# Half-pair units in the recurrent layer of a four-layer network, their chunks beside the preparation of the next unit

## The chip, the cores and the metric

One core of one Trainium2 chip runs the whole network in one launch, all in float32 (large products are split into a rounded part and a remainder, three matmuls for one). The metric is the device time of one execution in microseconds (us). Before the change it is 4200.47 us, the median of 3 runs (4192.66 to 4201.72).

## The reference, cut to what matters

The part that the change touches is the mixing of the first layer. From the projection `p` of 1024 tokens it computes two things side by side: a recurrence over 8 heads of 64 channels, and attention of 8 heads over a band of nine 64-token chunks.

```python
w = -softplus(-(w0 + tanh(p_wd) @ w2)) - 0.5;  decay = exp(-exp(w))
a = sigmoid(a0 + p_ad @ a2)
kk = normalised(heads(k * k_k));  k = k * (1 + (a - 1) * k_a)
def step(state, inp):                 # over 1024 tokens, for each head
    sa = einsum('bhvk,bhk->bhv', state, a_t)
    state = state * w_t + sa[..., None] * b_t + v_t[..., None] * k_t
    return state, einsum('bhvk,bhk->bhv', state, r_t)
y = groupnorm(y) * lnx_g + lnx_b + sum(r * k * r_k) * v
...
y_a = y * silu(gate_a)
y_b = chunk_attention(q_b, k_b, v_b, att_bias) * silu(gate_b)
h + concatenate([y_a, y_b]) @ w_out
```

Shifted `p_r, p_k, p_v` (each token minus its predecessor, times a factor, added back) feed the recurrence. The three layers behind it are not touched.

## The kernel before, in words

The kernel writes five instruction queues by hand: PE (TensorE), DVE (VectorE), ACT (ScalarE), POOL (GpSimd) and SP, which issues DMAs. Each queue runs in order. Each engine's program is a Python generator that yields at the end of a round; `weave` takes one round of each of several generators in turn, `chain` puts generators one behind the other, and `pace(main, other, steps, rounds)` lays `steps` rounds of `other` evenly over `rounds` rounds of `main`. All engines use the same pattern, so that round n of one meets round n of the others; a semaphore wait in a round holds everything queued behind it on that engine.

The stage after the projection is `pace(*_rwkv(), *_band(), BAND_STEPS, RW_ROUNDS)`: the recurrence as the main part, the band attention as the other. Two heads (128 channels) are a pair, numbered c = 0 to 3. The recurrence works on 64-token chunks. For each pair it has these parts:

- `*_early(c)` (6 rounds): token shift of K, R and V, and the normalisation of kk. For pair 0 it lies in the projection, for the others beside the second half's chunks of the pair before.
- `*_late(c)` (6 rounds), alone: decay and `a` by two small matmuls and sigmoids, a scan along the tokens (L2677), three exponentials (L1728, L1733, L1736), some ten products on DVE, and transposes of the operands through PSUM. All operate on 1024 tokens at once.
- `*_factor(c, g)` (13 rounds) for each half g of the tokens: the chunk matrices (L796, L808), five doubling steps that invert them (L818, L826, L832, with copies and adds by ACT and DVE and masks by POOL), and from them WT and U0.
- `*_chunks(c, g)` (16 rounds): eight chunks in sequence. The state goes PE (L877) to DVE (L2811) to PE (L888) to DVE (L2818) and from there to the next chunk's L877. L897 and L900 give the output.
- `*_tail(c)` (10 rounds): the bonus of pair c, and normalisation, gate and transposes of the output of pair c-1.

They are put together so, for every engine: late(c); factor(c, 0) woven with tail(c); chunks(c, 0) woven with factor(c, 1); chunks(c, 1) woven with early(c+1). With the rounds that `weave` adds this is 6 + 14 + 17 + 17 = 54 rounds for a pair. The band attention has 4 pairs of 8 query tiles, each tile 6 rounds (192 in all): scores (L917), bias and maximum (L2837, L2848), exponential (L1824), division (L2858), transposes (L644), product with V (L938).

PSUM has eight banks. A `Banks` ring deals them out in order, and who opens one waits until what used it before has been copied out: the recurrence has four (`for_rw`), the band four (`for_band`). SP loads the rows that the projection spilled to memory: `sp_raw(c)` three raw rows for early(c), `sp_qk`, V and gates for the band; two of the four pieces of the output weight are loaded while the projection ends. After the stage, `*_even` finishes pair 3 and starts the output product (L656 to L658); there POOL splits the first weight piece (L3584) before it does the tail of pair 3 (L3497, L3502, L3508, L3515).

Of the kernel before, what the change touches and what calls it, by code (L numbers as in the profile page):

```python
# [151 lines left out]
def run(gen):  # L152
    for _ in gen:
        pass
# [24 lines left out]
def build(nc, T, out):  # L179
    ctx = ExitStack()  # L180
    with ctx:
# [97 lines left out]
        RW_ROUNDS, BAND_STEPS = 212, 192  # L279
# [27 lines left out]
        def ring(first, n):  # L307
# [4 lines left out]
        for_rw, for_band = ring(0, 4), ring(4, 4)  # L312
# [8 lines left out]
        rwv = area([(n, 1024) for n in ("A", "SIG", "CS", "EX", "T1")] + [("RA", 2048), ("BN", 1024)] +  # L321
                   [(n, 1024) for n in ("R", "K", "KK", "BT", "KTL", "VN", "LT")] +
                   [("ROWS", HALF), ("LVL", 7 * 64), ("MASK2", 2 * 64), ("IDC", 64), ("WT0", 512),
                    ("WT1", 512), ("W2", 512), ("ST", P), ("WC", 16), ("BON", 16)], WORK, WORK_N)
        A, SIG, CS, EX, T1, BN, R, K, KK, BT, KTL, VN_R, LT = (rwv[n] for n in (
            "A", "SIG", "CS", "EX", "T1", "BN", "R", "K", "KK", "BT", "KTL", "VN", "LT"))
# [8 lines left out]
        KN, AN = T1, KK  # L335
        Am, AL, Fm, Gm, Ym = R[:, 0:HALF], R[:, HALF:], K[:, 0:HALF], K[:, HALF:], A[:, 0:HALF]
        X0, UU = Am, SIG[:, 0:HALF]
# [21 lines left out]
        def gn(b):  # L359
# [3 lines left out]
        handed = [(SIG[:, HALF:SEQ], rwv["WT0"], by8(WS0[:, 0:1024]), by8(WS0[:, 1024:2048])),  # L363
                  (A[:, HALF:SEQ], rwv["WT1"], by8(CS), by8(EX))]
# [34 lines left out]
        V_B, GATE_B, BONV, RRK = (XF[:, i * 1024:(i + 1) * 1024] for i in range(4, 8))  # L399
        GATE_R, LB = WS1[:, 0:1024], WS1[:, 1024:2048]  # L400
# [5 lines left out]
        def less_at(c):  # L406
            return LB if c else VN_R

        def raw_in(c, g):
            return done("raw", c, g) if c else done("ev", "proj", "rkv", g, 0, 1)  # L410
# [286 lines left out]
        def pe_proj():  # L697
            early = pe_early(0)
# [23 lines left out]
        def pe_early(c):  # L722
            ring = for_rw if c else every
            yield from nothing(3)
            for hf in range(2):
                b = ring.open("rwkv", "norm", c, hf)
                pe.wait_ge(*ring.free("rwkv", "norm", c, hf))
                pe.wait_ge(*done("rwkv", "kk_sq", c))
                E.matmul(b[:, :], head_ones[:, :], BT[:, hf * HALF:(hf + 1) * HALF], start=True,
                         stop=True).then_inc(*rw.pe.mark("rwkv", "norm", c, hf))  # L730
            yield from nothing(3)

        def pe_late(c):
            for hf in range(2):
                sl = slice(hf * HALF, (hf + 1) * HALF)
                for lo, what in ((0, "sig"), (64, "a")):
                    b = for_rw.open("rwkv", what, c, hf)
                    pe.wait_ge(*for_rw.free("rwkv", what, c, hf))
                    pe.wait_ge(*done("rwkv", "lora_ready"))
                    pe.wait_ge(*done("rwkv", "w_lora2"))  # L740
                    E.matmul(b[:, :], W2[lo:lo + 64, c * P:(c + 1) * P], LT[lo:lo + 64, sl], start=True,
                             stop=True).then_inc(*rw.pe.mark("rwkv", what, c, hf))
            yield
            for hf in range(2):
                pe_transposes(rw, for_rw, ("v_tr", c, hf), [KTL[:, (hf * 4 + i) * P:(hf * 4 + i + 1) * P]
                                                            for i in range(4)], done("rwkv", "shift", c, 2))
            yield from nothing(3)
            for what, src, ready in (("a_tr", RA[:, :, 0, :], "ra"), ("b_tr", tile_pairs(SIG), "ops"),
                                     ("k_tr", tile_pairs(A), "ops")):
                if what == "b_tr":  # L750
                    yield
                for hf in range(2):
                    pe_transposes(rw, for_rw, (what, c, hf), [src[:, hf * 4 + i, :] for i in range(4)],
                                  done("rwkv", ready, c))
            yield

        def pe_tail(c, R_):
            if c < 4:
                b = R_.open("rwkv", "bonus", c)
                pe.wait_ge(*R_.free("rwkv", "bonus", c))  # L760
                pe.wait_ge(*done("rwkv", "rk", c))
                for t in range(NT):
                    mm = E.matmul(b[:, 2 * t:2 * t + 2], RRK[:, t * P:(t + 1) * P], head_ones[:, 0:P:64], start=True,
                                  stop=True)
                mm.then_inc(*rw.pe.mark("rwkv", "bonus", c))
            yield from nothing(8)
            if c:
                pe_y_tr(c - 1, R_)
# [16 lines left out]
        def pe_factor(c, grp):  # L785
            U0, WT, AKT, ABT = handed[grp % 2]
            for h in range(2):
# [3 lines left out]
                pe.wait_ge(*done("rwkv", "ops", c))  # L791
# [71 lines left out]
        def pe_chunks(c, grp):  # L863
            U0, WT, AKT, ABT = handed[grp % 2]
            for i in range(4):
# [3 lines left out]
                for ch in range(2):  # L869
# [3 lines left out]
                    b = for_rw.open("rwkv", "us", c, n)  # L873
                    pe.wait_ge(*for_rw.free("rwkv", "us", c, n))
# [4 lines left out]
                    b = for_rw.open("rwkv", "ys", c, n)  # L879
                    pe.wait_ge(*for_rw.free("rwkv", "ys", c, n))  # L880
# [3 lines left out]
                    b = for_rw.open("rwkv", "kv", c, n)  # L884
                    pe.wait_ge(*for_rw.free("rwkv", "kv", c, n))
# [4 lines left out]
                b = for_rw.open("rwkv", "yo", c, t)  # L890
                pe.wait_ge(*for_rw.free("rwkv", "yo", c, t))
# [51 lines left out]
        def pe_even():  # L943
            after(pe, rw)
            after(pe, band)
            run(pe_tail(4, every))
# [616 lines left out]
        def act_proj():  # L1563
            after(act, begin)
            early = act_early(0)
# [132 lines left out]
        def act_early(c):  # L1698
            yield from nothing(2)
            act.wait_ge(*done("rwkv", "kk", c))  # L1700
            if c:
                act.wait_ge(*done("rwkv", "abt", c - 1, 1, 1))
            S.activation(BT, KK, ACT.Square).then_inc(*rw.act.mark("rwkv", "kk_sq", c))
            yield
            yield
            for func, scale, by in ((ACT.Ln, NORM_SCALE ** 2, None), (ACT.Exp, -0.5, "unit")):
                for hf in range(2):
                    e = BT[:, hf * HALF:(hf + 1) * HALF]
                    act.wait_ge(*(rw.act.last() if by else done("ev", "rwkv", "norm", c, hf)))
                    S.activation(e, e, func, scale=scale).then_inc(*rw.act.mark(*("rwkv", by, c, hf) if by else ()))  # L1710
            yield
            yield
# [2444 lines left out]
```

## Time and profile before

| | |
|---|---|
| median of 3 runs | 4200.47 us |
| time of the profiled execution | 4195.6 us |
| its span, first to last instruction | 4193.3 us |
| mean granted TensorE clock | 0.961 |
| busy: PE, DVE, ACT, POOL | 3890.8, 1708.3, 1363.4, 1297.4 us |

In the profile a line such as L877 is a line of the kernel file; lines of helpers (L644 transposes, L1490 and L2421 copies out of PSUM, L656 to L658 split products) serve many tiles. A float32 matmul appears as two records. "Granted clock" is TensorE's clock as a share of 2.4 GHz; a stretch at 1.2 GHz counts as 0.5.

### The profile page before, as it was taken

To read this page: it belongs to the slowest core of one execution; us is meant where nothing else is said; L and a number is where in the kernel's file an instruction comes from. 1 tells how busy PE (TensorE), PEld (TensorE's weight loads), DVE (VectorE), ACT (ScalarE), POOL (GpSimd) and SP (SyncE) were. 2 spreads that over 40 slices of the span, in tenths; PEclk is the share of its full clock that TensorE was granted. 3 is DMA by queue.
4 is the path that set the end of the run, shared out by engine and by line. 5 is a ranking of instruction groups with operands and counts; after the bars stand their busy time and mean duration, and the time that the engine had idled before them with its cause. 6 is when DMAs were issued, how large, how long until landed. Compare 5 with 4: busy or idle time off the path is not lost.

```text
span 4193.3 us, 59802 instructions
## 1 busy us (share of the span) xinstructions
PE 3890.8 (93%) x26332; PEld 3288.4 (78%) x26332; DVE 1708.3 (41%) x2714; ACT 1363.4 (33%) x2239; POOL 1297.4 (31%) x636
## 2 busy tenths in 40 slices
PE   8998867876999999999999989999999999999997
PEld 6887756765998898767587777897878988888877
DVE  2101566565231247753214464332187332332344
ACT  4122344333231243563222254222176212212133
POOL 3221221322113456672133101334102523323254
PEclk9999987877999999999999999999999999999998
DMA  3223010001111122000111100121100211111111
GB/s 110 95 96 136 2 43 37 8 18 73 41 41 40 41 71 61 26 21 31 38 46 48 41 1 16 56 101 33 42 10 21 71 60 51 41 51 51 50 41 41
DMA packets 156691, 199.12 MB, mean 47 GB/s; under 512 B 8848, under 2 KB 136720, under 8 KB 156432
## 3 DMA queue, kind: packets, MB, share of 16 engines
q1 hardware_dynamic: 156432, 195.30, 14.1%
q8 instruction: 207, 3.39, 0.3%
q14 instruction: 52, 0.43, 0.0%
HBM read 171.69 MB, written 23.59 MB: 47 GB/s over the span
## 4 chain that ended last, share of the span: by engine, by line
PE 77%; DVE 10%; ACT 6%; POOL 4%; issue 3%; DMA 0%; SPq 0%; POOLq 0%; ACTq 0%; DVEq 0%
PE pair L656 19%; PE pair L658 19%; PE pair L657 19%; PE pair L644 3%; PE pair L1160 1%; PE pair L1350 1%; PE pair L611 1%; POOL H L3642 1%; PE pair L826 1%; POOL W_r L3584 1%; PE pair L1320 1%; ACT BIG L2150 1%; PE pair L1200 1%; PE pair L818 1%; PE pair L938 1%
## 5 line engine op out<-in xcount | busy, mean ns | idle before, releaser
L656 PE MATMUL pair<-XT_r,W_r 128*128 128x512 f32 x2208 | 875.3, 396 | 8.6 <-ACT BIG L2088 1.9
L657 PE MATMUL pair<-BIG_r,W_r 128*128 128x512 f32 x2088 | 813.0, 389 | 0.0
L3584 POOL TENSOR_TENSOR W_r<-W,W_r 128x2048 fp32r<-128x2048 f32 (+2 forms) x91 | 402.7, 4425 | 997.2 <-ACT W_r L1500 997.1
L658 PE MATMUL pair<-XT_r,W_r 128*128 128x512 f32 x1696 | 660.8, 390 | 0.0
L656 PEld LDWEIGHTS pair<-XT_r,W_r 128*128 128x128 f32 x2208 | 414.9, 188 | 103.7 <-issue 10.8
L657 PEld LDWEIGHTS pair<-BIG_r,W_r 128*128 128x128 f32 x2088 | 392.3, 188 | 86.9 <-issue 7.0
L656 PE MATMUL pair<-W_r,BIG_r 128*128 128x256 f32 (+1 forms) x1280 | 417.9, 326 | 1.8 <-DVE MIX_r L2883 0.9
L658 PE MATMUL pair<-W_r,BIG_r 128*128 128x256 f32 (+1 forms) x1280 | 417.3, 326 | 0.0
L658 PEld LDWEIGHTS pair<-XT_r,W_r 128*128 128x128 f32 x1696 | 318.5, 188 | 67.0
L656 PE MATMUL pair<-W_r,XT_r 128*128 128x256 f32 x960 | 276.3, 288 | 3.8 <-POOL BIG_r L3758 2.2
L658 PE MATMUL pair<-W_r,MIX_r 128*128 128x256 f32 x960 | 271.6, 283 | 0.0
L656 PEld LDWEIGHTS pair<-W_r,BIG_r 128*128 128x128 f32 x1280 | 243.4, 190 | 22.3 <-issue 2.4
L658 PEld LDWEIGHTS pair<-W_r,BIG_r 128*128 128x128 f32 x1280 | 244.1, 191 | 20.0
L3758 POOL TENSOR_TENSOR BIG_r<-MIX,W_r 128x2048 fp32r<-128x2048 f32 x34 | 156.5, 4602 | 310.9 <-ACT W_r L2290 310.9
L1500 ACT ACTIVATE W_r<-W 128x2048 fp32r<-128x2048 f32 (+2 forms) x91 | 165.4, 1817 | 244.1 <-DMA W<-w_out 80.5
L657 PE MATMUL pair<-W_r,BIG_r 128*128 128x256 f32 x768 | 217.3, 283 | 0.0
L1490 ACT ACTIVATE BIG<-pair 128x512 f32<-128x512 f32 (+3 forms) x198 | 108.2, 557 | 325.4 <-PE pair L658 135.9
L658 PE MATMUL pair<-XT_r,BIG_r 128*128 128x512 f32 x544 | 212.2, 390 | 0.0
L3321 DVE TENSOR_TENSOR H<-H,pair 128x512 f32<-128x512 f32 x240 | 161.7, 686 | 121.0 <-PE pair L658 121.0
L657 PE MATMUL pair<-BIG_r 128*128 128x512 f32 x520 | 202.3, 389 | 0.0
L657 PE MATMUL pair<-W_r,XT_r 128*128 128x256 f32 x704 | 199.2, 283 | 0.0
L656 PEld LDWEIGHTS pair<-W_r,XT_r 128*128 128x128 f32 x960 | 184.9, 193 | 6.3 <-issue 2.5
(447 smaller groups left out, 7370.4 us busy)
## 6 DMA issues: line engine op xcount, KB each, us to landing
W<-w_in SPq DMA_DIRECT2D x29, 1024.0 KB, 5.5
W<-w_in_e SPq DMA_DIRECT2D x16, 1024.0 KB, 6.4
MIX<-w_up SPq DMA_DIRECT2D x15, 1024.0 KB, 5.3
MIX<-w_down SPq DMA_DIRECT2D x15, 1024.0 KB, 4.8
rows<-MIX SPq DMA_DIRECT2D x29, 512.0 KB, 7.7
W<-w_in_o SPq DMA_DIRECT2D x12, 1024.0 KB, 5.0
W<-w_in SPq DMA_DIRECT2D x17, 512.0 KB, 4.2
H<-x SPq DMA_DIRECT2D x16, 512.0 KB, 7.3
```

Source lines behind the costliest of these rows:

```text
L611: E.matmul(b[:, 0:P], ident[:, :], ident[:, :], start=True, stop=True)
L644: mm = E.transpose(b[:, i * P:(i + 1) * P], s, ident[:, :])
L656: E.matmul(b[:, 0:n], lh, rh, start=k == ks[0], stop=False)
L657: E.matmul(b[:, 0:n], lh, rl, start=False, stop=False)
L658: mm = E.matmul(b[:, 0:n], ll, rh, start=False, stop=k == ks[-1])
L818: mm = E.matmul(b[rows, sq(q)], AL[rows, sq(q)], Fm[rows, sq(q)], start=True, stop=True)
L826: mm = E.matmul(b[rows, sq(q)], Gm[rows, sq(q)], Ym[rows, sq(q)], start=True, stop=True)
L1490: S.activation(dst, R_.bank(st.name, *name)[:, 0:width], ACT.Copy, scale=scale).then_inc(*st.act.mark("ev", st.name, *name))
L1500: S.activation(WHI[k % 2][:, 0:n], WSTAGE[k % 2][:, 0:n], ACT.Copy).then_inc(*s_high.mark("high", k))
L3321: V.tensor_tensor(h, h, b, ALU.add).then_inc(*ff.dve.mark("ev", "mlp", "down", n, t, c0))
L3584: G.tensor_tensor(WLO[k % 2][:, 0:n], WSTAGE[k % 2][:, 0:n], WHI[k % 2][:, 0:n], ALU.subtract).then_inc(*s_split.mark("split", k))
L3758: G.tensor_tensor(WL[k % 2][:, :], staged[k % 2], WH[k % 2][:, :], ALU.subtract).then_inc(*st.pool.mark(st.name, "split", k))
```

## The change

The recurrence now runs in eight units, a pair c and a token half g each. Early and late work on 512 tokens of one half. The order for every engine is late(0, 0) and factor(0, 0); then, for each unit, its chunks woven with late and factor of the next unit, and with early of the unit after that; where a unit is the first of a pair, tail of the pair before follows early. That is 19 rounds and eight times 20, and `RW_ROUNDS` goes from 212 to 180. DVE's bonus product is a generator of its own at the start of each unit.

The PSUM banks are dealt anew: two for chunks alone, three for the rest of the recurrence, three for the band. Buffers are laid out anew. ACT takes the transposed v, a and b, DVE the transposed k. On SP, `sp_raw(1)` goes behind the projection's spills and waits for shifts of the second half, the first two pieces of the output weight are loaded after the stage, and POOL splits the first one behind three instructions of the last tail.

```diff
-        RW_ROUNDS, BAND_STEPS = 212, 192
+        RW_ROUNDS, BAND_STEPS = 180, 192
-        for_rw, for_band = ring(0, 4), ring(4, 4)
+        for_rw, for_chunk, for_band = ring(0, 3), ring(3, 2), ring(5, 3)
...
+        UNITS = [(c, g) for c in range(4) for g in range(2)]
+        def unit(c, g, ahead):
+            n = 2 * c + g + ahead
+            return UNITS[n] if 0 <= n < 8 else None
...
         def pe_rwkv():
             after(pe, proj)
-            for c in range(4):
-                yield from pe_late(c)
-                yield from weave(pe_factor(c, 0), pe_tail(c, for_rw))
-                yield from weave(pe_chunks(c, 0), pe_factor(c, 1))
-                yield from weave(pe_chunks(c, 1), pe_early(c + 1) if c < 3 else nothing(6))
+            yield from chain(pe_late(0, 0), pe_factor(0, 0))
+            for c, g in UNITS:
+                after_it, then = unit(c, g, 1), unit(c, g, 2)
+                yield from weave(pe_chunks(c, g), chain(pe_late(*after_it), pe_factor(*after_it)) if after_it else nothing(19),
+                                 chain(pe_early(*then) if then else nothing(6),
+                                       pe_tail(c - 1, for_rw) if c and g == 0 else nothing(10)))
...
-                    b = for_rw.open("rwkv", "us", c, n)
+                    b = for_chunk.open("rwkv", "us", c, n)
...
-        def act_late(c):
+        def act_late(c, g):
+            before = unit(c, g, -1)
             if c:
-                act.wait_ge(*done("rwkv", "yo", c - 1, NT - 1))
-                act.wait_ge(*done("ev", "rwkv", "us", c - 1, 15))
+                act.wait_ge(*done("rwkv", "yo", c - 1, 4 * g + 3))
+            if before:
+                act.wait_ge(*done("rwkv", "k_tr", *before))
...
-            S.activation(EX, CS, ACT.Exp, scale=-KAPPA).then_inc(*rw.act.mark("rwkv", "ex", c, 0))
+            S.activation(EX, CS, ACT.Exp, scale=-KAPPA).then_inc(*rw.act.mark("rwkv", "ex", c, g, 0))
...
+            yield from chain(dve_late(0, 0), dve_factor(0, 0))
+            for c, g in UNITS:
+                after_it, then = unit(c, g, 1), unit(c, g, 2)
+                yield from weave(dve_chunks(c, g), chain(dve_late(*after_it), dve_factor(*after_it)) if after_it else nothing(19),
+                                 chain(dve_early(*then) if then else nothing(6),
+                                       dve_tail(c - 1, for_rw) if c and g == 0 else nothing(10), dve_bonus(c, g)))
...
         def pool_even():
+            tail = pool_tail(3)
+            for _ in range(8):
+                next(tail)
             pool_split(EVEN_OUT)
-            run(pool_tail(4))
+            run(tail)
...
         def sp_first():
-                else:
-                    sp_chunk(EVEN_OUT + j + 2 - len(PROJ), T["w_out_e"][0], (j + 2 - len(PROJ)) * Q)
...
-                if j == 11:
-                    sp_raw(1)
+            sp_raw(1)
...
+            after(sp, rw)
+            for n in range(2):
+                sp_chunk(EVEN_OUT + n, T["w_out_e"][0], n * Q)
             after(sp, band)
```

## Rows read from the trace of the kernel before

**Rows 1.** The page: span, TensorE clock by slice, chain that ended last.

```profile
span 4193.3 us, 59802 instructions
...
PEclk9999987877999999999999999999999999999998
...
PE 77%; DVE 10%; ACT 6%; POOL 4%; issue 3%; DMA 0%; SPq 0%; POOLq 0%; ACTq 0%; DVEq 0%
```

**Rows 2.** Windows: us, then busy PE, PEld, DVE, ACT, POOL; clock, DMA share, GB/s.

```profile
401.30:1017.20 615.90, 480.27 (x7348) 403.78 (x7348) 369.72 (x736) 237.57 (x496) 133.14 (x114) 0.82 0.08 28
1017.20:1049.70 32.50, 5.82 (x29) 5.69 (x29) 19.59 (x19) 13.22 (x15) 14.11 (x5) 0.53 0.61 226
```

**Rows 3.** Windows of the four late parts: the first, and their sum.

```profile
401.30:427.60 26.30, 9.43 (x48) 7.01 (x48) 18.32 (x25) 11.12 (x18) 0.52 (x1) 0.61 0.60 220
...
sum 101.00, PE 41.36 PEld 29.25 DVE 75.36 ACT 45.80 POOL 0.81; mean PE 10.34 PEld 7.31 DVE 18.84 ACT 11.45 POOL 0.20
```

**Rows 4.** Windows of the four factor(c, 0) with tail: the first, their sum.

```profile
427.60:463.90 36.30, 29.67 (x703) 26.21 (x702) 16.84 (x35) 10.66 (x28) 9.30 (x7) 0.95 0.01 2
...
sum 169.20, PE 135.40 PEld 120.03 DVE 95.16 ACT 56.04 POOL 65.88; mean PE 33.85 PEld 30.01 DVE 23.79 ACT 14.01 POOL 16.47
```

**Rows 5.** Windows of the four chunks(c, 0) beside factor(c, 1): their sum.

```profile
sum 181.60, PE 169.63 PEld 148.19 DVE 104.56 ACT 69.29 POOL 44.17; mean PE 42.41 PEld 37.05 DVE 26.14 ACT 17.32 POOL 11.04
```

**Rows 6.** Windows of the four chunks(c, 1) beside early(c+1): the last, their sum.

```profile
980.70:1017.20 36.50, 32.37 (x246) 25.60 (x244) 16.28 (x48) 11.19 (x27) 2.93 (x5) 0.73 0.02 5
sum 164.10, PE 133.88 PEld 106.32 DVE 94.64 ACT 66.44 POOL 22.27; mean PE 33.47 PEld 26.58 DVE 23.66 ACT 16.61 POOL 5.57
```

**Rows 7.** Timeline of PE, pair 2: start and end of factor(2, 1).

```profile
775.62 0.80 PE L796 MATMUL pair<-BIG 64*64 64x64 f32 x26
...
813.78 1.10 PE L859 MATMUL pair<-BIG 64*64 64x64 f32 x29
```

**Rows 8.** Groups by line, whole stage, DVE: count, busy us, mean ns, idle before.

```profile
L2677 DVE TENSOR_TENSOR_SCAN BIG<-BIG 128x512 f32<-128x512 f32 x8 | 9.5, 1222 | 98.4 <-ACT BIG L1723 98.4
L2683 DVE SCALAR_TENSOR_TENSOR BIG<-BIG 128x1024 f32<-128x1024 f32 x4 | 4.9, 1225 | 0.1
L2789 DVE TENSOR_TENSOR BIG<-BIG,pair 128x512 f32<-128x512 f32 x40 | 27.5, 688 | 43.6 <-PE pair L826 43.6
L2848 DVE TENSOR_REDUCE STAT<-H 128x1 f32<-128x640 f32 (+4 forms) x64 | 38.5, 642 | 0.2
```

**Rows 9.** ACT's table loads: timeline in late(2), and one group by line.

```profile
706.30 1.28 ACT L1723 ACT_TABLE_LOAD   x1 [2.32 <-PE pair L741]
707.60 2.42 ACT L1723 ACTIVATE BIG<-pair,PAR 128x512 f32<-128x512 f32 x4
710.04 1.28 ACT L1727 ACT_TABLE_LOAD   x1
...
L1710 ACT ACT_TABLE_LOAD x6 | 7.7, 1283 | 0.1
```

**Rows 10.** Groups by line, whole stage: state matmul of the chunks, band scores' copy.

```profile
L877 PE MATMUL pair<-BIG 128*128 128x128 f32 x128 | 34.4, 356 | 27.7 <-DVE BIG L2818 25.0 <-DVE BIG L2782 2.7
L1817 ACT ACTIVATE H<-pair,PAR 128x384 f32<-128x384 f32 (+2 forms) x48 | 22.7, 524 | 30.4 <-PE pair L917 30.4
```

**Rows 11.** The chain in order of time at the stage's start.

```profile
402.94 9.03 DMA XT<-rows
```

**Rows 12.** Timeline at the stage's end.

```profile
1027.53 1.22 DVE L2741 TENSOR_TENSOR MIX<-MIX,STAT 128x1024 f32<-128x1024 f32 x1
...
1030.88 4.50 POOL L3584 TENSOR_TENSOR W_r<-W,W_r 128x2048 fp32r<-128x2048 f32 x1 [15.45 <-ACT W_r L1500]
1035.34 2.97 POOL L3497 TENSOR_TENSOR MIX<-MIX,PAR 128x1024 f32<-128x1024 f32 x1
...
1040.47 2.34 POOL L3508 TENSOR_TENSOR MIX<-MIX,XT 128x1024 f32<-128x1024 f32 x1
...
1045.79 2.35 POOL L3515 TENSOR_TENSOR MIX<-MIX,W 128x1024 f32<-128x1024 f32 x1 [2.98 <-DVE MIX L2421]
```

More of the change, by code:

```diff
@@ L720, in pe_proj, with pe_early @@
             run(early)
-        def pe_early(c):
-            ring = for_rw if c else every
+        def pe_early(c, g):
+            ring, hs = for_rw if c else every, token_half(g)
             yield from nothing(3)
[L725 to L730, printed above, removed]
-            yield from nothing(3)
@@ L733, in pe_late @@
[L733 to L742, printed above, removed]
+            b = ring.open("rwkv", "norm", c, g)
@@ new lines, in pe_late @@
+            yield
+            pe_transposes(rw, for_rw, ("b_tr", c, g), [tile_pairs(SIG)[:, i, :] for i in range(4)], done("rwkv", "ops", c, g))
+            pe_transposes(rw, for_rw, ("k_tr", c, g), [tile_pairs(A)[:, i, :] for i in range(4)], done("rwkv", "ops", c, g))
+            b = for_rw.open("rwkv", "bonus", c, g)
+            pe.wait_ge(*for_rw.free("rwkv", "bonus", c, g))
+            pe.wait_ge(*done("rwkv", "rk", c, g))
+            for i in range(4):
+                mm = E.matmul(b[:, 2 * i:2 * i + 2], four(RRK, g)[:, i, :], head_ones[:, 0:P:64], start=True, stop=True)
@@ L755, in pe_late @@
+            mm.then_inc(*rw.pe.mark("rwkv", "bonus", c, g))
             yield
         def pe_tail(c, R_):
[L758 to L765, printed above, removed]
@@ L945, in pe_even @@
             after(pe, band)
-            run(pe_tail(4, every))
+            run(pe_tail(3, every))
             order = (4, 5, 6, 7, 0, 1, 2, 3)
@@ L1704, in act_early @@
             yield
             yield
[L1706 to L1710, printed above, removed]
+            act.wait_ge(*done("ev", "rwkv", "norm", c, g))
@@ L1763, in act_rwkv @@
             after(act, proj)
-            for c in range(4):
-                yield from act_late(c)
-                yield from weave(act_factor(c, 0), act_tail(c, for_rw))
-                yield from weave(act_chunks(c, 0), act_factor(c, 1))
-                yield from weave(act_chunks(c, 1), act_early(c + 1) if c < 3 else nothing(6))
+            yield from chain(act_late(0, 0), act_factor(0, 0))
+            for c, g in UNITS:
+                after_it, then = unit(c, g, 1), unit(c, g, 2)
+                yield from weave(act_chunks(c, g), chain(act_late(*after_it), act_factor(*after_it)) if after_it else nothing(19),
+                                 chain(act_early(*then) if then else nothing(6),
+                                       act_tail(c - 1, for_rw) if c and g == 0 else nothing(10)))
         def act_y_tr(c, R_):
@@ L1802, in act_chunks @@
                     act.wait_ge(*done("rwkv", "ys", c, n))
-                    S.activation(YN[rows, t, :], for_rw.bank("rwkv", "ys", c, n)[rows, 0:P], ACT.Copy).then_inc(
+                    S.activation(YN[rows, t, :], for_chunk.bank("rwkv", "ys", c, n)[rows, 0:P], ACT.Copy).then_inc(
                         *rw.act.mark("ev", "rwkv", "ys", c, n))
@@ L3516, in pool_tail @@
+            for half in range(2):
+                pool.wait_ge(*done("ev", "rwkv", "y_tr", c, half))
+            G.tensor_tensor(Y, Y, GATE_R, ALU.mult).then_inc(*rw.pool.mark("rwkv", "gated", c))
             yield
@@ L3519, in pool_rwkv @@
             after(pool, proj)
-            for c in range(4):
-                yield from nothing(6)
-                yield from weave(pool_factor(c, 0), pool_tail(c))
-                yield from weave(nothing(16), pool_factor(c, 1))
-                yield from weave(nothing(16), pool_early(c + 1) if c < 3 else nothing(6))
+            yield from chain(nothing(6), pool_factor(0, 0))
+            for c, g in UNITS:
+                after_it, then = unit(c, g, 1), unit(c, g, 2)
+                yield from weave(nothing(16), chain(nothing(6), pool_factor(*after_it)) if after_it else nothing(19),
+                                 chain(pool_early(*then) if then else nothing(6),
+                                       pool_tail(c - 1) if c and g == 0 else nothing(10)))
         def pool_factor(c, grp):
```

390 lines of the change are left out of this document (189 added, 201 removed).

## The prediction, written before the changed kernel had run

> **What bounds the kernel now.** I read the page first. The chain that ended last is 77% PE, and the clock by slice dips to 7 and 8 tenths only in slices 6 to 10, between about 400 and 1020 us [rows 1]. So everything outside that stretch is TensorE at work at full clock, and the change touches nothing there but its two edges. The stretch is the recurrence with the band. I then cut it by windows at the starts of L741, L796 and the chunks of each pair. It lasts 615.9 us with PE busy 480.3, DVE 369.7, ACT 237.6 and POOL 133.1, at a mean clock of 0.82 [rows 2]. No engine is full: the stage is bound by how its parts follow each other.
>
> The windows by part tell them apart. The four late parts take 101.0 us, with PE busy 41.4 and DVE 75.4 [rows 3]: one serial chain in which DVE does nearly all. The four factor(c, 0) take 169.2, the first of them, which has no tail beside it, 36.3 [rows 4]. Chunks beside factor take 181.6 us with PE busy 169.6, so 93%: this part alone is bound by PE [rows 5]. Chunks beside early take 164.1 [rows 6]. The four sums make 615.9. The last two rows show the waste: the chunks that have a factor beside them take 45.4 us a time, those without 41.0, so a factor beside the chunks costs 4 us where one alone costs 36 to 44. Before, half of the factors and all late parts stand alone. Afterwards only those of unit (0, 0) do.
>
> **The change part by part.** The sum is made against the profiled execution: 4195.6 us, of which 4193.3 is span; the median of the runs, 4200.5, is 4.9 above it. A difference under 0.2% (8 us) is no difference that a measurement of this kernel can tell.
>
> 1. Start: late(0, 0) and factor(0, 0), before 26.3 + 36.3 = 62.6 us [rows 3, 4]. In both kernels the first band tile in PE's queue waits for rows that land at 412.0 [rows 11], and late goes on only then. Behind that, some nine DVE operations go from 1024 to 512 wide. The 1024-wide one takes 1.225 us, the 512-wide one 0.688 [rows 8], so 9 x 0.54 = 4.8 less; two exponentials and half of the transposes and copies save some 3 more. I take 54.6, say 55. SP now has `sp_raw(1)`, three rows of 0.5 MB, ahead of the band's rows at that point and lacks one weight piece of 1 MB; 0.5 MB more at the 220 GB/s of this window [rows 3] is 2 us. That is left to the waits in item 5.
>
> 2. Units with a next one, seven of them, 20 rounds each. Rounds 1 to 6 hold late (half), early (half), three chunks and 6.4 band rounds. I count DVE, which bounds late. Late: a scan of 1.22, ten operations at 0.69, one at 0.4, a copy of 0.69, two small ones at 0.16, in all 9.5 us. Early: five at 0.69 and one at 0.5, 4.0. Bonus 0.7. Three chunks of 0.29 + 2 x 0.28 and the outputs, 3.1. Band: a tile costs DVE 3.4 us (its largest term is L2848, 38.5 us over 32 tiles [rows 8]), times 1.07 tiles 3.7. Together 21.0, and 2 for waits that nothing fills: 23 us. It could not be under 17, the serial chain of a half late alone (25 less 8), and could be 38, if late takes its 25 and the chunks' turns do not overlap it (rival below). I take 23, because before DVE was idle for a quarter of late and the added work can lie there.
>
>    Rounds 7 to 20 hold factor, five chunks and 2.2 band tiles. Factor(2, 1) with chunks beside it went from 775.6 to 814.9, 39.3 us [rows 7], with nearly 13 chunk rounds where now ten lie beside it, and somewhat more band. I take 38; below is 36.3, factor without chunks [rows 4], above is 45.4, the whole part with chunks [rows 5]. A unit is then 61, and seven are 427.
>
> 3. Tail. Beside factor(c, 0) it costs (169.2 - 36.3) / 3 - 36.3 = 8.0 us each [rows 4]: POOL's masks and DVE's adds of the doubling steps are queued behind tail operations. It stays beside factor for three pairs, a few rounds later and partly in the rounds without chunks. I take 6, so 18; the ends are 0 and 24.
>
> 4. The last unit has only chunks and the band. Before, 36.5 us for 17 rounds with 15.4 band rounds [rows 6]; now 20 with 21.3. In proportion to the band it would be 50, with the chunks' share unchanged 42. I take 46.
>
> 5. Waits added by the banks. With three banks, the band's near scores wait until ACT has copied the far ones out (L1817) of the same tile; with four it was an older bank. L1817 takes 0.52 us [rows 10], for 24 tiles that have far keys; behind it on PE wait the chunks. Ends: 0 and 24 x 1.5. Two banks for chunks: the next ys waits for the yo of two chunks before, which DVE adds before it adds the us anyway, so nothing. Three banks at the start of factor: the last akt group waits for the first mask product of DVE, where the chunks waited before. I take 8 for all, with the 2 us of SP.
>
> 6. ACT switches its function table 20 times in the stage before: six at L1710, the rest at sigmoid, exponential and root. In halves, sigmoid and the return from it come 16 times for 8, logarithm and exponential of early 12 for 6: 34 in all, 14 more at 1.28 us [rows 9], 18 us of an engine that is busy 238 of 616. Per unit this gives ACT some 16 us in rounds 1 to 6, under DVE's 21, so I leave it in the 2 us of item 2.
>
>    The row shows the load at 706.30 and its first activation at 707.60, with nothing between [rows 9]. The Trainium skill (ScalarE: Activation LUTs, section What ACT_TABLE_LOAD costs) gives a switch about 2.66 us, as a drain of 1.38 comes with the load. By that page the 14 switches would cost 37 us of ACT and not 18; no drain is seen in this row as a gap of its own, and the sum goes by the row.
>
> The stage: 55 + 427 + 18 + 46 + 8 = 554, which is 62 less than 615.9.
>
> 7. Behind the stage, 32.5 us until the output product starts [rows 2]. The last tail's operand is ready at 1027.53 + 1.22 = 1028.8, but POOL does the weight split first and starts L3497 at 1035.34 [rows 12]. Moved behind three tail operations, this gains 6.6. The split (4.50) now lies where POOL waits 2.98 for the transposes, before L3515, and 1.5 of it stand out. Net 5 less. It turns to nothing if the weight piece, now loaded only after the stage, is late: before, ACT rounded it at 1028.8, 11.6 us after the stage, and 2 MB at the window's 226 GB/s take 9 [rows 2]. The reload of H is queued behind it by the same 9 us.
>
> The other rows that SP loads (raw rows of pairs 2 and 3) are issued when the band ends a pair, at band rounds 48 and 96, that is 14 and 9 rounds before early asks for them; six rows of 0.5 MB take 14 us at 220 GB/s, and nine rounds last 27. They stay hidden.
>
> Total: 4195.6 - 62 - 5 = 4128.6, and I forecast 4130.
>
> **The rivals.** First: TensorE becomes the bound and the units run as dense as chunks beside factor do now. For it speaks that this was the one part at nearly full clock. All PE work at full clock is 480.3 x 0.82 = 394 us; start and last unit keep 101 us with some 64 of it, the other 330 at 93% busy [rows 2, 5] are 353: stage 454, and 4195.6 - 162 - 5 = 4029. Against it: DVE's 21 us in six rounds, where PE has little to do, so the clock may fall again there.
>
> Second: the added waits bite. The near scores' wait holds PE, and the table loads hold ACT in front of chunk outputs; with 24 x 1.3 and half of the 18 us on the path, 31 + 9 - 8 = 32 more, 4161. For it speaks that L1817 already waits 30 us in the stage for its scores, so ACT reaches them in step with PE [rows 10]; against it, that ACT is idle for 60% of the time.
>
> Third, on the other side: rounds 1 to 6 don't overlap. In PE's queue the chunk's L877 and L888 alternate with late's transposes, and each waits for DVE or ACT, which in turn hold late's results behind the chunk's. L877 already waits 25 us for L2818 [rows 10]. If halving saves late nothing (25.2) and six chunk rounds add their 36.5 / 17 each, 13, the rounds take 38, a unit 76: 532 + 127 = 659 for the stage, 4195.6 + 43 - 5 = 4234. It decides from a unit of (615.9 + 5 - 127) / 7 = 70.6 us on. Against it: factor is just such a chain of PE, ACT and DVE, and it did take the chunks in for 4 us.
>
> Fourth: table switches cost more than their rows show. Late's exponentials stand on the unit's serial chain, and each switch could bring a gap of up to a second load's length with it (1.28 [rows 9]). With 14 more switches that is 14 x 1.28 = 18 on the path, 4148. Against it: the row of late(2) shows no gap between load and activation [rows 9]. The Trainium skill (ScalarE: Activation LUTs, same section) has a rule for such a gap, the drain of 1.38 us; by it this rival would give 4148 too, within a microsecond or two.
>
> **How the numbers follow.** Forecast 57% (own range 4100 to 4155), denser 10%, added waits 16%, no overlap 10%, table drains 7%. The range of 8 in 10 takes half of the way to the denser case and most of the dear ones: 4075 to 4185. Faster by over 0.2% are all but the no-overlap case and a thin rest between: 0.87; same 0.03; slower 0.10.
>
> **What would show it.** Right: windows from one unit's first L796 to the next are 58 to 65 us, DVE busy over 70% of them, mean clock of the stage over 0.88, stage 530 to 580 us. The table loads are 34. L3497 starts at once after L2741 in the last tail. Wrong: units over 70 us with L877 waiting mainly for late's operations on DVE; or PE waiting at L917 for L1817 more than 20 us in all; or POOL waiting for raw rows; or units near 50 us with PE over 90% busy. If the changed stage is no shorter though it has fewer rounds, the count of rounds says nothing and each round has grown.

## The result: slower, and the profile after

The changed kernel took 4238.4 us (median of 4 runs, 4233.7 to 4249.9) against 4199.3 us for the kernel before, measured beside it: a ratio of 1.0104, with a 95% interval of 1.009 to 1.0118. Forecast were 4130 us, in a range of 4075 to 4185. The profiled execution took 4238.8 us.

The page of the changed kernel (span, granted clock in 40 slices, chain that ended last by engine) looks much like that of before [rows 1]: the same 77% PE, and a dip of the clock that now fills slices 5 to 11, where it was 6 to 10.

```profile
span 4237.1 us, 59916 instructions
...
PEclk9999878777899999999999999999999999999998
...
PE 77%; DVE 9%; ACT 6%; POOL 4%; issue 3%; DMA 0%; SPq 0%; POOLq 0%; DVEq 0%; ACTq 0%
```

The windows tell more (columns as in [rows 2]). The first runs from the stage's start to the end of the recurrence, the second from there to the output product; they answer to the two of [rows 2]. The third holds the seven units with a next one. The fourth and the fifth are rounds 1 to 6 and rounds 7 to 20 of the first of them, and the last line is the last unit.

```profile
401.30:1022.20 620.90, 487.36 (x7218) 408.18 (x7218) 364.00 (x771) 246.43 (x508) 132.31 (x116) 0.80 0.08 28
1022.20:1090.30 68.10, 25.05 (x161) 20.19 (x159) 31.67 (x46) 25.69 (x41) 18.80 (x12) 0.62 0.40 141
462.50:985.30 522.80, 419.46 (x6300) 352.50 (x6298) 323.08 (x672) 215.24 (x434) 121.34 (x105) 0.81 0.06 22
462.50:488.60 26.10, 16.21 (x112) 11.50 (x110) 19.95 (x38) 17.35 (x30) 2.38 (x4) 0.80 0.00 1
488.60:534.70 46.10, 42.28 (x805) 36.94 (x804) 25.76 (x58) 14.16 (x32) 11.00 (x12) 0.89 0.01 2
...
985.30:1022.20 36.90, 30.31 (x202) 23.78 (x200) 15.03 (x45) 12.54 (x32) 0.29 (x2) 0.68 0.00 1
```

A unit takes 522.8 / 7 = 74.7 us where 61 were forecast, or 63.6 with the tails' share. The recurrence is 5.0 us longer than the stage before (620.9 against 615.9), and the output product starts 68.1 us behind it instead of 32.5.

What fills these 68 us stands in the timeline (start, us, engine, line, operation, count; in brackets the idle time before and who ended it):

```profile
1029.54 2.37 PE L656 MATMUL pair<-ident,H 128*128 128x128 f32 x10 [4.55 <-DVE H L2855]
...
1041.88 2.37 PE L656 MATMUL pair<-ident,H 128*128 128x128 f32 x10 [4.18 <-DVE H L2855]
...
1056.20 2.40 PE L940 MATMUL pair<-H,XT 128*64 128x128 f32 x20 [0.61 <-DVE H L2860]
...
1071.54 1.23 DVE L2732 TENSOR_TENSOR MIX<-MIX,STAT 128x1024 f32<-128x1024 f32 x1
...
1073.03 2.73 POOL L3491 TENSOR_TENSOR MIX<-MIX,PAR 128x1024 f32<-128x1024 f32 x1 [11.59 <-DVE MIX L2732]
...
1081.94 4.52 POOL L3579 TENSOR_TENSOR W_r<-W,W_r 128x2048 fp32r<-128x2048 f32 x1
1086.42 2.34 POOL L3506 TENSOR_TENSOR MIX<-MIX,XT 128x1024 f32<-128x1024 f32 x1
...
1090.29 0.40 PE L668 MATMUL pair<-W_r,BIG_r 128*128 128x256 f32 x1 [2.52 <-DVE MIX_r L2880]
```

Once the recurrence's last matmuls are through at 1025, band tiles run with nothing beside them until 1061: `pace` hands over at most one band round per round of the recurrence, and there are now 180 of those for 192 band rounds. Before, there were more rounds than band rounds. Twelve are left over, two tiles' worth. Neither the forecast nor any rival saw it, though it stands in the diff; the forecast even counted 6.4 band rounds in six rounds and 21.3 in twenty, more than one a round.

Also new are some of PE's waits over the stage (engine, tile and line, releaser: us in total, times, longest). In the list of before, PE never waited in the places of the first and the last, and 3.5 us in that of the second.

```profile
PE pair L919 <- ACT H L1814: 20.7, 21, 2.6
...
PE pair L888 <- DVE BIG L2808: 15.3, 13, 2.6
...
PE pair L810 <- DVE W L2777: 10.8, 8, 2.4
```

L919 are the near scores, which wait until ACT has copied the far scores out of the bank; L810 is factor's akt group, which waits for the first mask product. Both come from the smaller rings: with the old banks in the changed kernel (below) neither is in the list of PE's waits. The table loads are 34, by count as forecast; the largest two groups by line (busy, mean ns, idle before):

```profile
L1725 ACT ACT_TABLE_LOAD x8 | 10.3, 1283 | 1.5 <-PE pair L750 1.4
...
L1729 ACT ACT_TABLE_LOAD x8 | 10.3, 1283 | 0.1
```

### The profile page after: what moved, and what is told of

Same layout as the page of the kernel before. It is cut to its first block, busy times and chain, and to the rows that moved or that the text cites. A ratio compares the mean times of both kernels' runs of the same rounds, so it can differ in the third digit from the quotient of the medians.

```text
span 4237.1 us, 59916 instructions
## 1 busy us (share of the span) xinstructions
PE 3919.7 (93%) x26332; PEld 3309.3 (78%) x26332; DVE 1716.1 (41%) x2782; ACT 1388.2 (33%) x2280; POOL 1301.0 (31%) x648
## 4 chain that ended last, share of the span: by engine, by line
PE 77%; DVE 9%; ACT 6%; POOL 4%; issue 3%; DMA 0%; SPq 0%; POOLq 0%; DVEq 0%; ACTq 0%
PE pair L668 19%; PE pair L670 19%; PE pair L669 19%; PE pair L656 3%; PE pair L1162 1%; PE pair L1352 1%; PE pair L623 1%; PE pair L828 1%; POOL H L3637 1%; POOL W_r L3579 1%; PE pair L1322 1%; ACT BIG L2147 1%; PE pair L1202 1%; DVE H L2962 1%; PE pair L940 1%
## 5 line engine op out<-in xcount | busy, mean ns | idle before, releaser
L670 PEld LDWEIGHTS pair<-W_r,MIX_r 128*128 128x128 f32 x960 | 184.9, 193 | 0.0
```

What stands on the lines that cost most here:

```text
L670: mm = E.matmul(b[:, 0:n], ll, rh, start=False, stop=k == ks[-1])
```

## The experiments

Ratios are against the kernel before, run beside each.

**The band rounds left over.** The changed kernel, with one edit in `pace`:

```
-        b = next(other, "end") if (r + 1) * steps // rounds > r * steps // rounds else None
+        b = None
+        for _ in range((r + 1) * steps // rounds - r * steps // rounds):
+            b = next(other, "end")
```

> The changed kernel, but where 192 band rounds are laid over 180 rounds of the recurrence, one of them may carry two, so that none is left over. In the changed kernel at most one is carried, and 12 rounds of the band (two tiles), with the end of a third, run alone from 1022 to 1061 us. Theory A (these left-over tiles are a cost of their own): the 36 us go, two tiles come back beside the recurrence at about 5 us each, so about 4212 us, and the output product's first L668 comes at 1065 instead of 1090. Rival (every round of band costs the same wherever it lies, the units have simply grown): 4230 to 4242.

It took 4221.4 us, ratio 1.0059 (1.0042 to 1.0075): 17 less than the changed kernel. The two tiles had ended 39 us behind the recurrence, but less than half of that comes back. The seven units take 522.5 us as before. The start grows from 61.2 to 66.0, the last state matmul comes at 1027.8 instead of 1020.9, and one tile still ends behind the recurrence.

**The band's own fourth bank, alone.** The kernel before, with one bank less for the band and nothing else:

```
-        for_rw, for_band = ring(0, 4), ring(4, 4)
+        for_rw, for_band = ring(0, 4), ring(4, 3)
```

> The kernel before, with the band's ring cut from four banks to three and the eighth bank unused; nothing else. Theory B (the third bank makes the near scores wait on PE for ACT's copy of the far ones, which in the changed kernel shows as PE L919 waiting 20.7 us for L1814 in the stage): 24 waits of about 0.9 us, most of them on the path, 4212 to 4220. Rival (the waits fall where PE would be idle anyway): 4196 to 4204.

4215.6 us, ratio 1.0041 (1.0026 to 1.0056): 16 us for one bank. PE's waits name it, once for each of the 24 tiles with far keys:

```profile
PE pair L917 <- ACT H L1817: 17.9, 24, 1.6
```

**The old banks in the changed kernel.**

```
-        for_rw, for_chunk, for_band = ring(0, 3), ring(3, 2), ring(5, 3)
+        for_rw, for_band = ring(0, 4), ring(4, 4)
+        for_chunk = for_rw
```

> The changed kernel with the banks dealt as before: four shared by chunks and the rest of the recurrence, four for the band. Theory B: the PE waits for L1814 (20.7 us) and for the first mask product L2777 (10.8 us) go, 4210 to 4220 with the left-over band tiles still there. Rival (chunks need banks of their own when late and factor open banks between theirs; a shared ring makes chunk matmuls wait for copies of late): slower than the changed kernel, 4245 to 4280.

4205.6 us, ratio 1.0017 (1.0007 to 1.0026), 33 less than the changed kernel, twice what the band's bank alone explains. Rounds 7 to 20, from factor's first matmul to its last, fall from 48.2 us in the mean to 44.4; rounds 1 to 6 stay at 26.5.

**Late ahead of the chunks.** The changed kernel with late of the next unit in rounds of its own, on every engine, 211 rounds, so that no band round is left over:

```
-                yield from weave(pe_chunks(c, g), chain(pe_late(*after_it), pe_factor(*after_it)) ...
+                yield from pe_late(*after_it) if after_it else nothing(6)
+                yield from weave(nothing(17), pe_chunks(c, g), pe_factor(*after_it) ...
```

> The changed kernel in half units and with its banks, but late of the next unit stands alone ahead of the chunks and is not woven with them; factor, early and tail stay woven; 211 rounds instead of 180, so no band rounds are left over. Theory D (late and chunks don't overlap in the in-order queues, six rounds with both cost as much as late alone plus the chunk rounds): no slower than the run with the left-over rounds removed, 4190 to 4215. Rival (the overlap of late and chunks is worth the 9 us a unit that a half late alone takes beyond what it adds beside chunks): 4250 to 4290.

4236.0 us, ratio 1.0093 (1.0077 to 1.0108): 15 over the kernel with the repaired `pace`, so neither expectation held. That is 2 us a unit for the weaving, with the small rings; the next runs look at it without the band, and then with the old banks.

**The recurrence by itself.** In the kernel before, the band runs first and the recurrence after it, so that each has its own stretch. The extra time of the whole is no matter here; the stretch is.

```
-            run(pace(pe_rwkv(), pe_band(), BAND_STEPS, RW_ROUNDS))
+            run(chain(pe_band(), pe_rwkv()))
```

> The kernel before, with the same instructions for the band and for the recurrence, but the whole band first and the recurrence behind it, on every engine; SP's row loads are reordered so, and POOL's mask gets one more wait on its own queue. It gives the recurrence by itself. All theories: the band alone, at the 12.3 us a tile that the left-over tiles show in the changed kernel, takes 32 x 12 = 390 us; the recurrence about 4 x (22 + 36 + 38 + 28) = 496, so some 4460 to 4500 us in all.

The same cut of the changed kernel:

> The changed kernel cut in the same way: band first, recurrence in half units behind it (one more wait of DVE on itself ahead of the state's memset). Theory E (half units overlap as planned when nothing else is in the queues, and the loss comes from banks, left-over rounds and the band in between): the recurrence is at least 50 us shorter than in the same cut of the kernel before, about 7 x 52 + 50 + 26 = 440. Rival F (late and chunks hold each other whatever else runs): within 20 us of it.

They took 4406.7 us (1.0493, 1.0466 to 1.052) and 4430.1 us (1.0549, 1.0529 to 1.0569). The windows of the first: the whole recurrence, and late(0), both halves at once.

```profile
712.40:1217.00 504.60, 371.11 (x6406) 316.21 (x6404) 266.04 (x481) 131.86 (x238) 119.63 (x78) 0.82 0.06 20
...
712.40:735.50 23.10, 8.67 (x42) 6.34 (x40) 17.10 (x17) 10.71 (x14) 2.35 (x1) 0.64 0.00 0
```

And of the second: the seven units, the whole recurrence, and late(0, 0), one half.

```profile
788.20:1225.90 437.70, 352.33 (x5612) 302.65 (x5610) 241.80 (x483) 140.20 (x245) 108.12 (x78) 0.75 0.05 13
...
739.90:1250.50 510.60, 403.09 (x6399) 346.35 (x6398) 269.10 (x542) 155.79 (x275) 120.62 (x87) 0.76 0.04 12
...
739.90:755.30 15.40, 6.26 (x33) 4.86 (x30) 9.23 (x14) 7.69 (x11) 2.34 (x1) 0.71 0.00 1
```

This is the main result. Without the band, and without any band bank in play, the new order of the recurrence is not shorter than the old: 510.6 against 504.6 us. A unit takes 437.7 / 7 = 62.5 us with no band in it. Two half lates are 2 x 15.4 = 30.8 us of chain where one whole one is 23.1.

Two things besides the order differ between the stretches. The second still has the rings of three and two, and L810 waits 8.2 us in it, which nothing did in the first; its clock is 0.76 against 0.82. So the order alone may be a few us better than the old one, but nowhere near the 50 that its expectation asked for. The cut kernel with the old banks was not run.

The band alone, 401.3 to 712.4 and 401.3 to 739.9, is 28 us longer in the second. With its three banks PE waits 16.9 us at L919 for the far copy, 24 times, and with four not at all; the rest of the 28 was not taken apart.

**Woven or not, with the band out of the way.** The previous kernel with late not woven, as above:

> The cut of the changed kernel, with late of the next unit ahead of the chunks and not woven with them. A half late alone takes 15.4 us there (739.9 to 755.3), six rounds of it with chunks and early 24. Theory D (late and chunks gain nothing from lying side by side): recurrence 490 to 515 us, total 4410 to 4435. Rival (the overlap hides the three chunks and early): recurrence 530 to 560, total 4450 to 4480.

```profile
786.60:1225.00 438.40, 338.32 (x5573) 294.37 (x5570) 235.09 (x475) 141.36 (x242) 102.89 (x77) 0.79 0.04 12
```

From the end of the first factor to the end of the last, the seven units take 438.4 us so and 437.7 woven. This flatters the kernel without weaving: two chunk steps of its seventh unit come behind the last factor. From the end of the first factor to the last state matmul it takes 468.1 us (786.6 to 1254.7) against 459.6 (788.2 to 1247.8). So the weaving saves 8.5 us in all, a little over 1 us a unit. The whole took 4443.9 us (1.0581, 1.0566 to 1.0595), 14 more than woven; the rest is not in this stretch and is open. And with the band paced in, the old banks and the repaired `pace`:

> Old banks, no left-over band rounds, late ahead of the chunks and not woven with them. Against the same with late woven (4181 us). Theory D: 4175 to 4190. Rival (the overlap is worth the 15 us that it was worth with the new banks): 4192 to 4206, no better than the kernel before.

4185.0 us, ratio 0.9962 (0.9949 to 0.9976), beside 4181.2 for its woven fellow (next), a difference that the intervals can't tell from none. Late beside chunks is worth 0 to 2 us a unit in the three comparisons (nothing that can be told with the old banks, 1 in parts, 2 with the new banks), where the forecast counted on most of a late.

**Both repairs in the changed kernel** (`pace` and banks):

> The changed kernel with both repairs: banks as before (four shared, four for the band) and no left-over band rounds. If the two causes add, 4238 - 33 - 17 = 4188, 11 under the kernel before. If the doubled band rounds cost more among tighter units, 4195 to 4206.

4181.2 us (6 runs), ratio 0.9961 (0.9948 to 0.9974): faster than the kernel before. The two causes add, and a little more: 4238.4 - 17 - 33 = 4188. Its seven units:

```profile
459.20:946.80 487.60, 402.96 (x6331) 339.11 (x6327) 323.16 (x678) 220.94 (x446) 120.71 (x105) 0.84 0.07 23
```

Even here the band ends last: the last tail begins (DVE L2718) at 998.91, 14 us behind the last chunk's output, where before it began right behind it.

**Banks 2, 2 and 4.** The kernel with the repaired `pace`, and the fourth bank back for the band alone:

```
-        for_rw, for_chunk, for_band = ring(0, 3), ring(3, 2), ring(5, 3)
+        for_rw, for_chunk, for_band = ring(0, 2), ring(2, 2), ring(4, 4)
```

> The changed kernel without left-over band rounds, and with the banks dealt 2 for chunks, 2 for the rest of the recurrence, 4 for the band. It separates the two halves of the old deal. If the band's fourth bank alone was worth the 40 us between the run without left-over rounds and the one with the old banks too: 4181 to 4190. If only its own wait goes (16 us, as when the kernel before lost that bank), and the recurrence's waits for masks and late's copies stay or grow with two banks: 4200 to 4225.

4237.0 us, ratio 1.0086 (1.0072 to 1.01), outside what either side expected, and 16 more than with 3, 2 and 3. The wait moved to factor, where it was 13.4 us with 3, 2 and 3:

```profile
PE pair L812 <- DVE W L2779: 21.0, 8, 2.7
```

With four for the band both times, a shared ring of four is 56 us better than two rings of two (4181.2 against 4237.0). A split that takes from either side is paid for.

**The clock.** Four kernels add matmuls whose results nobody reads, to keep PE's granted clock up. Two have 14 a unit (28 records of the trace) ahead of late's transposes, one on the repaired kernel and one on the changed kernel cut in parts. Two more have 38 a unit (76 records), ahead of early's norm (from pair 1 on) and factor's first product too.

```
+        KEEP_UP.update({("rwkv", what, c, g): n for c in range(4) for g in range(2) if (c, g) != (0, 0)
+                        for what, n in (("a_tr", 6), ("b_tr", 8))})
```

> The run with both repairs, plus dummy matmuls on PE in rounds 4 to 6 of each unit (6 ahead of the a transposes, 8 ahead of the b transposes, 28 records of 128 columns), where PE waits for DVE's products anyway. Theory C (factor starts at a low clock because the six rounds before it leave PE thin: granted clock 0.58 to 0.82 there in the changed kernel, and the first 12 us of its factor part run at half speed): 3 to 4 us a unit back, 20 to 28 in all against the same kernel without them. Rival (the dummies stand in front of the chunks' matmuls and cost what they give): within 8 us of it, or slower.

> The cut of the changed kernel (band first, recurrence in half units behind it), plus 28 records of dummy matmuls of 128 columns a unit ahead of late's a and b transposes. In the cut, the recurrence takes 510.6 us; the first 16.3 us of a factor part run at a granted clock of 0.50, and the same two rounds take 7.2 us more there than in the cut of the kernel before, which is at 1.00. Theory C: the clock is up when factor starts, 5 to 7 us a unit, the recurrence 465 to 480 us, the total 4385 to 4400. Rival (dummies delay the chunks queued behind them as much, or the clock falls anyway): 4420 or more.

> The cut of the changed kernel with more dummy matmuls: 8 ahead of early's norm, 10 and 12 ahead of late's a and b transposes, 8 ahead of factor's first product (76 records of 128 columns a unit). With 28 records the clock rose at 807 us and had fallen again by 818. Theory C (the low clock at factor's start costs the cut 5 to 7 us a unit): the start now runs at 1.00 and the recurrence is 20 us or more shorter, total 4410 or less. Rival (the clock matters little there, since each step waits for DVE, and dummies cost their own time): 4425 to 4450.

> The same 76 records a unit in the version with both repairs (old banks, no left-over rounds; 4181 us without dummies, 4178 with 28 records). Theory C: 4160 or less. Rival: 4175 to 4195, the first two factor rounds no shorter at clock 1.00 than at 0.77, as the version with 28 records already shows in one unit (12.2 us at 1.00 against 12.1 at 0.77).

With 28 in the repaired kernel: 4178.0 us, ratio 0.9946 (0.9933 to 0.9959), 3 less than without, which the intervals can't tell from none. Its seven units:

```profile
460.20:944.40 484.20, 401.03 (x6526) 340.27 (x6523) 322.83 (x678) 219.96 (x446) 120.37 (x105) 0.90 0.07 23
```

The clock rose from 0.84 to 0.90. Factor's start in the first unit, from its first product to the second state matmul behind it, went from 12.4 us to 11.8. The windows of 12.1 and 12.2 us that an expectation above compares do not end at the same instruction. Timeline of PE, first without the added matmuls, then with them:

```profile
482.93 1.29 PE L801 MATMUL pair<-BIG 64*64 64x64 f32 x26
...
495.37 0.39 PE L882 MATMUL pair<-BIG,W 128*128 128x128 f32 x2
```

```profile
484.80 0.80 PE L803 MATMUL pair<-BIG 64*64 64x64 f32 x26
...
496.61 0.39 PE L884 MATMUL pair<-BIG,W 128*128 128x128 f32 x2
```

In parts, 28 records gave 4430.6 us (1.0548, 1.0533 to 1.0562), no change, and 510.6 us for the recurrence as without. But inside a unit much moves. These are rounds 1 to 6 and rounds 7 to 20 of the second unit, first without and then with the 28:

```profile
851.40:873.50 22.10, 13.24 (x70) 9.31 (x70) 16.29 (x30) 12.82 (x19) 2.08 (x2) 0.67 0.21 71
873.50:913.00 39.50, 36.62 (x730) 33.31 (x730) 16.51 (x39) 6.49 (x15) 10.16 (x8) 0.80 0.01 3
```

```profile
851.70:876.50 24.80, 17.19 (x100) 13.68 (x100) 16.24 (x30) 12.81 (x19) 2.08 (x2) 0.72 0.20 64
876.50:912.20 35.70, 31.44 (x730) 28.55 (x730) 17.52 (x39) 6.38 (x15) 10.15 (x8) 0.95 0.01 3
```

The same work of factor and chunks is 3.8 us shorter at the higher clock, and rounds 1 to 6, where the added matmuls stand, are 2.7 longer. Over the seven units it is 12 us less and 12 more; in the repaired kernel 8 less and 5 more.

The 76 records cost: 4448.1 (1.0594, 1.0573 to 1.0616) in parts, 18 more, and 4205.0 (1.0009, 0.9999 to 1.0019) in the repaired kernel, 24 more by the median (4191.1 to 4206.1). In its profiled execution, the shortest, rounds 7 to 20 are 12 us shorter in all and rounds 1 to 6 are 33 longer. So the low clock does cost something, 1 to 2 us a unit in rounds 7 to 20, but added matmuls pay as much or more for it in rounds 1 to 6. What the low clock costs in rounds 1 to 6 themselves, these runs can't tell from the added matmuls' own time.

## Why the prediction was wrong

Against the profiled execution, 4238.8 - 4128.6 = 110 us are missing. By place: start +6, units +78, last unit -9, item 5's 8 us that are in the units' own windows -8, from the recurrence's end to the output product 68.1 - 27.5 = +41, elsewhere +3.

By cause, as the medians of the runs show it: 17 us are the band rounds left over, 40 the banks (4221.4 - 4181.2), and the other 51 (4181.2 - 4130) remain in the repaired kernel. There the units are 487.6 - 445 = 43 of them: 22 in rounds 1 to 6 (26.1 us in the mean against 23), 18 in the three units with a tail (rounds 7 to 20 take 50.0 against 38 + 6) and 3 in the four others, whose 38.8 are near the 38 of the forecast.

**Item 2 is the step that failed**: a unit of 61 us. Rounds 1 to 6 were to take 23 us, because late could lie beside three chunks at almost no cost. They took 26.5 in the mean, and rounds 7 to 20 took 48.2 (52.8 with a tail, 44.7 without) against 38. Without a tail, rounds 7 to 20 take 44.0 with the repaired `pace` alone and 38.8 with the old banks too: their excess is the banks', which item 5 had at 8 us. Two more things were wrong in item 2.

First, the sum was by DVE's busy time, and the band was paid only as its 3.7 us of DVE. The recurrence alone, with tails, already needs 62.5 us a unit, near the 63.6 that the forecast gave to recurrence, tails and band together. With the band in the queues a unit takes 7 (69.7, repaired) to 12 more (74.7).

Second, the serial chains hardly overlap where each has turns on the same in-order engines. Chunks by themselves, at the end of the kernel before in parts, start every 2.04 us (timeline of PE, the state matmuls alone):

```profile
1200.61 0.49 PE L877 MATMUL pair<-BIG 128*128 128x128 f32 x2
...
1202.65 0.49 PE L877 MATMUL pair<-BIG 128*128 128x128 f32 x2 [0.68 <-DVE BIG L2818]
...
1204.69 0.49 PE L877 MATMUL pair<-BIG 128*128 128x128 f32 x2
```

Beside late, in the changed kernel in parts, they start 8 us apart, at 789.41, 797.05 and 805.14. The timeline from the first to the second shows how:

```profile
789.08 1.28 ACT L1725 ACT_TABLE_LOAD   x1
790.37 1.27 ACT L1725 ACTIVATE BIG<-pair,PAR 128x512 f32<-128x512 f32 x2
791.09 1.23 DVE L2677 TENSOR_TENSOR_SCAN BIG<-BIG 128x512 f32<-128x512 f32 x1 [5.87 <-ACT BIG L1725]
792.23 0.26 DVE L2809 TENSOR_TENSOR BIG<-pair,BIG 64x128 f32<-64x128 f32 x1
792.55 0.48 PE L888 MATMUL pair<-BIG 64*128 64x128 f32 x2 [1.99 <-DVE BIG L2809]
...
794.25 0.74 DVE L2644 SCALAR_TENSOR_TENSOR BIG<-W,PAR,H 128x512 f32<-128x512 f32 x1
795.04 1.36 DVE L2655 TENSOR_SCALAR BIG<-BIG,PAR 128x512 f32<-128x512 f32 x1
...
796.32 0.58 DVE L2816 SCALAR_TENSOR_TENSOR BIG<-BIG,pair 64x64 f32<-64x64 f32 x2
797.05 0.77 PE L879 MATMUL pair<-BIG,W 128*128 128x128 f32 x2 [3.80 <-DVE BIG L2816]
```

DVE sat idle for 5.87 us, not for want of work but because the scan at the head of its queue waited for ACT's sigmoid (L1725), with a table load ahead of it. The chunk's add, L2809, 0.26 us, stood behind it, and PE's L888 waited 1.99 us for that. Then five operations of late and early go ahead of the state update L2816, and PE's L879 waits 3.80. The forecast had read the idle quarter of DVE during late as room; it is time in which the queue's head waits, and nothing behind it can use it. Late alone and three chunks alone would be 15.4 + 3 x 2.04 = 21.5 us, with the chunks at full clock. Woven, they take 22.1 with early (the second unit, under The clock above) and 18.0 in the seventh unit, which has no early (1165.5 to 1183.4). Halving, on the other hand, costs 7.7 us of chain a pair.

The third rival described this mechanism, and its 4234 us is near the time. It put 15 us a unit on it, though, all in rounds 1 to 6; in fact the unit grew by 11 to 14, mostly in rounds 7 to 20, and part of the total is leftover band and banks. The number is closer than its reasons. The second rival's near scores that wait for the far copy are there at 20.7 us, but its 4161 lacked the rest. The first is refuted: PE is busy for 419.5 of 522.8 us, 80%, and was never the bound. The fourth: 34 loads of 1.283 us, and no gap between load and activation, as in [rows 9]. But eight of them, where it was four, stand at the start of late as at 789.08 above: the product L750 is ready at 789.5 and the sigmoid starts at 790.37. That is about 0.9 us on the chain, and no run prices it.

The other items:

- Item 1: 61.2 us against 55; before 62.6. The half late is 15.4 alone, but the first band tile, with rows that land at 412, and later waits took most of the saving. It fell to 57.9 in the repaired kernel.
- Item 3: a tail costs 52.8 - 44.7 = 8.1 us, 24 for three, at the upper end of 0 to 24, and as before, 8.0 [rows 4]. In the repaired kernel it is 50.0 - 38.8 = 11.2, so 34 for three, above that range.
- Item 4: the last unit took 36.9 against 46. It carried 20 band rounds of the 21.3 assumed, so scaling by the band was too dear.
- Item 5: 8 us stood for what measures 40. Its upper end for the band, 24 x 1.5 = 36, held that part (16 in the kernel before). The wrong part was that the last akt group would wait only "where the chunks waited before": L810 waits 10.8 us that nobody waited before, and with the repaired `pace` this goes from 13.4 with 3, 2 and 3 to 21.0 with 2, 2 and 4, one bank less.
- Item 6: count and length right; not all hidden, as said of the fourth rival.
- Item 7: from the last tail's first operation (1061.57) to the output product 28.7 us, before 32.1 (1017.56 to 1049.67), so 3.4 less against 5. L3491 starts 0.26 us after L2732, as forecast [rows 12].

Open is what makes the repaired kernel 19 us faster than before. Item 7 is 3.4 of it. Late beside chunks is at most 4 of it, since the kernel without that takes 4185.0. The chunks beside factor(c, 0) and a more even spread of the band remain, and no run tells them apart.

## What to carry to other kernels

Fewer rounds are no time saved: where two serial chains share in-order engines, idle time of an engine can be used only if its queue's head isn't the one that waits, so time each chain by itself, cut apart, before weaving them. When a loop that carries another one along gets shorter, count whether it still carries all of it. A bank taken from a ring that is in use turns into a wait of PE on a copy; measure it in the old kernel first, where it is one edit.

## What the hardware showed besides

In parts, the start of a factor (columns as in [rows 2]) had a granted clock of 0.50, though PE was busy 15.3 of 16.3 us:

```profile
811.80:828.10 16.30, 15.28 (x217) 13.91 (x216) 6.51 (x14) 1.64 (x4) 5.36 (x4) 0.50 0.01 2
```

From the first L798 there (811.77) to the second L879 behind it (828.15) it is 16.4 us. With 76 records a unit the same stretch, L804 to L885, is 13.7 us (814.06 to 827.76). The matmuls ran at the higher clock in its first and last thirds: a group of 32 as in L828 took 1.10 us instead of 1.92.

The clock also counts in a chain that goes to and fro between PE and DVE. Chunks alone ran 2.04 us apart above; there the clock was 1.00. In the last unit of the changed kernel in parts it was 0.50 from 1234.7 to 1238.1, and the chunks run 3.3 us apart, with matmuls of 0.77 us and more in place of 0.49 (timeline of PE):

```profile
1234.73 0.77 PE L879 MATMUL pair<-BIG,W 128*128 128x128 f32 x2 [0.78 <-DVE BIG L2816]
...
1238.07 0.79 PE L879 MATMUL pair<-BIG,W 128*128 128x128 f32 x2
```

L2655, a DVE operation of 512 columns, took 1.36 us from 795.04, beside a POOL operation of 1.04 us that began at 795.08; L2644 just ahead of it took 0.74. The DVE operation that began at 799.33 (L2692), beside the next POOL operation, took 1.31.
